# Mixer input projection as two panels of seven half-size products each

## The chip, the cores and the metric

The kernel runs on one core of a Trainium2 chip. The metric is device time in microseconds (us) of one execution of the whole program; the median of several executions is given with the lowest and the highest. The profile that is read below is of one further execution.

## The reference, cut to what matters

The program computes a block with a mixer (a gated linear attention beside a pooling branch), a mixture of 32 experts, and a second, two-layer block. The change touches one matrix product near the start, the mixer's input projection. `h` has 512 tokens, the context `hc` has 256, both with 1024 features.

```python
p_x = modulate(rmsnorm(h, norm_mix_w[l]), sh1, sc1) @ w_in[l]
p_c = modulate(rmsnorm(hc, norm_mix_w[l]), csh1, csc1) @ w_in[l]
q, k, v, g, r_f, r_b, pool_in = jnp.split(p, SPLIT_POINTS, axis=-1)
# widths: q 256, k 256, v 512, g 512, r_f 16, r_b 16, pool_in 512
gk_f = jax.nn.log_sigmoid((r_f @ w_gk_f + b_gk_f)) / GATE_NORMALIZER
```

Of the context only k, v and the two r are used. The same stage also needs the modulation vectors, `silu(c) @ w_ada + b_ada`, with `w_ada` of 1024 x 6144, of which 4096 columns are read here.

## The kernel before

Every weight comes through `ring`, a ring of slots of 1 MB each (128 partitions x 2048 floats). In this stage eight slots are used. The list of tiles is fixed when the program is built: `stream.add` appends a tile, tile n goes into slot n mod 8, and SyncE issues its load (`Stream.load`, line 188) as soon as tile n-8 has been given back. TensorE takes tiles in order with `take`; `release` gives the oldest back with a matmul, `owe` leaves that to the next `release` or `settle`, `keep` holds a tile a step longer. Tiles 0 to 7 are w_ada for the first modulation vectors, tiles 8 to 11 are w_in columns 0 to 1023 (q, k, then v), tile 12 is the upper half of w_in for g, 13 to 16 are w_ada, 17 is the lower half for g, 18 to 21 are w_ada, 22 to 31 are the same for the pooling input.

All of it is issued on SyncE's queue (q1 in the profile). GpSimd issues three transfers on its own queue (q0): x and ctx at the start and, at line 733, one store of 20352 KB of zeros to `y_scratch` in HBM, which is needed much later, by the experts. All queues use the same 16 DMA engines.

The stage runs on TensorE in this order. The normalised rows are transposed and written as `hT` (features on partitions, 512 + 256 columns). `project` (line 388) then goes over the eight feature chunks of 128, and for each over its output banks in PSUM, with one float32 matmul each (the profile counts each float32 matmul as two):

- q and k: four banks of 512 tokens and two of 256 context tokens; then the narrow product with `wr` (line 891) for r, and its copy `rT`;
- v: six banks (four of tokens, two of context). Ahead of feature chunks 1 to 4, `gates(i)` (line 902) puts in two small products of rT, into banks 0 and 1, which VectorE empties into `zb` (line 823);
- g: four banks; the pooling input: four banks. Ahead of each of their 16 feature chunks stands one step of `vector_step` (line 543): four matmuls side by side on quarters of the array, which multiply one w_ada tile by the vector.

ScalarE and VectorE empty the banks. ScalarE also turns `zb` into exponentials (lines 773 to 777, then `act_power`), VectorE scans it, and `dve_shift` and `dve_scale` make the operands of the gated linear attention, which starts in the next block, behind a barrier of all engines.

A product in seven parts is used in this kernel already, later, in the two last layers. One 1024 x 1024 weight panel, as four blocks of 512 x 512 named 11, 12, 21, 22, times 512 tokens in two halves of 256: instead of eight half-size products there are seven (`Panel`: p1, p2, p6, p7, p5, p4, p3), whose operands are four sums of feature quarters (`Sums`: s1 to s4) and four sums of weight blocks (`weights_t3`, `t2`, `t4`, `t1`, in place in the ring, lines 488 to 508). `channel_product` (line 453) is one such product with channels on partitions, 16 matmuls of 256 columns; `token_product` (line 440) has tokens on partitions, 8 matmuls of 512 columns.

## Time and profile before

| | us |
|---|---|
| median of 3 runs (lowest, highest) | 2169.72 (2169.31, 2170.83) |
| time of the profiled execution | 2184.99 |
| its span | 2182.8 |
| the stage of the change, on TensorE | 47.97 to 207.68 |

Times of instructions are in us from the start of the span. "Idle before" is the time in which the engine had nothing to do, with what ended it behind the arrow. In a window a digit such as PEclk 1.00 is the share of TensorE's full clock (2.4 GHz) that was granted, and DMA share is the mean busy share of the 16 DMA engines.

### The profile page before, as it was taken

What the parts mean: (1) busy time and instruction counts of PE and PEld (TensorE: products, weight loads), DVE (VectorE), ACT (ScalarE), POOL (GpSimd) and SP (SyncE); (2) the same over time, 40 slices, a digit from 0 to 9 for tenths busy, and PEclk for the clock granted to TensorE, in tenths of its full rate; (3) what the DMA queues carried; (4) which work ended last, traced back from release to release, by engine and by line L of the source; (5) the groups of instructions that cost most, each with busy time, mean ns of one, the idle gap of its engine ahead of it and who ended that gap; (6) DMA issues with size and microseconds to landing.
All of it is one profiled execution on the core that took longest, in us unless ns stands there. A gap on an engine that the chain in (4) does not pass through costs nothing.

```text
span 2182.8 us, 35887 instructions
## 1 busy us (share of the span) xinstructions
PE 2114.5 (97%) x14889; PEld 1141.3 (52%) x14889; DVE 950.8 (44%) x1640; ACT 491.0 (22%) x876; POOL 216.2 (10%) x266
## 2 busy tenths in 40 slices
PE   5999899999999999999999999899999999999998
PEld 2434545344444544444354443588584448777643
DVE  1041625833223223322322344754577625597742
ACT  2030312111101101110110110311126102666560
POOL 1000001121121122112112232200000000000000
PEclk9999999999999999999999999999999999999999
DMA  9957137999999999999999999723121032212200
GB/s 378 351 193 258 61 119 315 422 415 400 409 410 407 414 413 409 416 413 415 411 416 413 410 420 419 292 78 109 39 101 54 1 105 79 97 58 97 97 20 38
DMA packets 111830, 565.88 MB, mean 259 GB/s; under 512 B 16933, under 2 KB 29010, under 8 KB 77938
## 3 DMA queue, kind: packets, MB, share of 16 engines
q1 hardware_dynamic: 88950, 512.93, 58.4%
q0 software_dynamic: 19584, 49.84, 6.4%
q10 hardware_dynamic: 3228, 2.17, 0.3%
q8 instruction: 47, 0.77, 0.1%
q14 instruction: 21, 0.17, 0.0%
HBM read 545.21 MB, written 37.62 MB: 267 GB/s over the span
## 4 chain that ended last, share of the span: by engine, by line
PE 80%; DVE 3%; DMA 3%; issue 1%; ACT 1%; ACTq 0%; SPq 0%; DVEq 0%; POOLq 0%
PE ps L2309 30%; PE ps L459 11%; PE ps L2279 11%; PE ps L3848 5%; PE ps L3747 4%; PE ps L2287 4%; PE ps L447 3%; PE ps L1533 2%; PE ps L3727 2%; PE ps L3279 1%; DMA ring<-in_w_gu 1%; PE ps L3270 1%; DMA ring<-in_odd_w_in 1%; PE ps L2899 1%; PE ps L2943 1%
## 5 line engine op out<-in xcount | busy, mean ns | idle before, releaser
L2309 PE MATMUL ps<-ring,xeT 128*32 128x512 f32 x6144 | 684.5, 593 | 3.0 <-issue 1.7
L2309 PEld LDWEIGHTS ps<-ring,xeT 128*32 128x32 f32 x6144 | 259.9, 110 | 392.4 <-issue 335.5
L2279 PE MATMUL ps<-ring,mT 128*32 128x512 f32 x2048 | 322.3, 592 | 0.0
L2287 PE MATMUL ps<-ring,mT 128*32 128x256 f32 x2048 | 264.1, 379 | 0.0
L2048 DVE TENSOR_TENSOR mT<-ps,spread_bias 128x768 f32<-128x768 f32 x32 | 30.6, 957 | 462.5 <-PE ps L2309 462.4
L1986 ACT ACTIVATE mT<-mT 128x768 f32<-128x768 f32 x32 | 27.0, 845 | 867.0 <-DVE mT L2048 838.4
L2287 PEld LDWEIGHTS ps<-ring,mT 128*32 128x32 f32 x2048 | 118.3, 110 | 96.7 <-issue 66.2
L459 PE MATMUL ps<-hT_late,ring 128*128 128x256 f32 x704 | 155.5, 379 | 1.1 <-issue 1.1
L2279 PEld LDWEIGHTS ps<-ring,mT 128*32 128x32 f32 x2048 | 122.9, 110 | 52.8 <-issue 9.2
L459 PEld LDWEIGHTS ps<-hT_late,ring 128*128 128x128 f32 x704 | 133.4, 190 | 22.2 <-issue 4.1
L3848 PE MATMUL ps<-ring,mT 128*128 128x512 f32 x256 | 110.4, 592 | 0.0
L1808 POOL DMA_INDIRECT xe<-xn_scratch,idx x93 | 96.6, 1038 | 30.6 <-issue 28.7
L1819 ACT ACTIVATE xeT<-xturned,modx 128x96 f32<-128x96 f32 x248 | 91.8, 453 | 9.7 <-PE ps L2309 9.7
L2075 DVE STREAM_TRANSPOSE mT<-mT 128x768 f32<-128x768 f32 x31 | 30.3, 978 | 142.0 <-PE ps L2287 141.9
L3848 PEld LDWEIGHTS ps<-ring,mT 128*128 128x128 f32 x256 | 48.6, 190 | 60.8 <-issue 60.7
L1839 POOL TENSOR_TENSOR mark<-cst 128x1 f32<-128x1 f32 x57 | 11.9, 210 | 686.9 <-DVE ysb L2087 643.8
L402 PE MATMUL ps<-ring,hT 128*128 128x512 f32 x160 | 71.7, 598 | 0.0
L402 PE MATMUL ps<-hT,ring 128*128 128x512 f32 (+1 forms) x160 | 64.5, 556 | 2.2 <-DVE vtok L840 1.5
L1533 PE MATMUL ps<-ring,mixT 128*128 128x512 f32 x128 | 56.7, 596 | 2.4 <-DMA ring<-in_w_out 1.2
L1922 POOL DMA_INDIRECT y_scratch<-ysb,y_idx x54 | 55.6, 1029 | 23.1 <-issue 23.1
L459 PE MATMUL ps<-mT,ring 128*128 128x256 f32 x256 | 56.6, 379 | 0.0
L3747 PE MATMUL ps<-ring,mT 128*128 128x512 f32 x128 | 55.3, 592 | 0.0
(497 smaller groups left out, 2467.6 us busy)
## 6 DMA issues: line engine op xcount, KB each, us to landing
ring<-in_w_gu SPq DMA_DIRECT2D x128, 2048.0 KB, 9.4
ring<-in_w_down SPq DMA_DIRECT2D x128, 1024.0 KB, 28.2
y_scratch<-zeros POOLq DMA_DIRECT2D x1, 20352.0 KB, 99.1
ring<-in_even_w_in SPq DMA_DIRECT2D x18, 1024.0 KB, 7.3
ring<-in_w_ada SPq DMA_DIRECT2D x32, 512.0 KB, 8.0
ring<-in_odd_w_in SPq DMA_DIRECT2D x16, 1024.0 KB, 6.7
ring<-in_w_ada SPq DMA_DIRECT2D x8, 1024.0 KB, 20.1
ring<-in_w_in SPq DMA_DIRECT2D x8, 1024.0 KB, 18.4
```

Of the source, the lines that this page charges most:

```text
L402: mm = nc.tensor.matmul(dst, left(k, w, kk), right(k, w, kk), start=first, stop=last)
L447: mm = nc.tensor.matmul(out, left[:, k, t * P:(t + 1) * P], w[:, k, :], start=fresh and k == 0 and (n == BANK or t == 0), stop=k == 3, ski ...
L459: mm = nc.tensor.matmul(out, w[:, k, c * P:(c + 1) * P], left[:, k, :], start=fresh and k == 0 and c % 2 == 0, stop=k == 3, skip_group_che ...
L1533: mm = nc.tensor.matmul(bank(j_out[t, h].bank), mixT[:, k, t * P:(t + 1) * P], tiles[k // 2][:, k % 2, h * BANK:(h + 1) * BANK], start=k = ...
L1808: nc.gpsimd.indirect_dma_start(xe[:, q * DQ:(q + 1) * DQ], None, quarter_rows, bass.IndirectOffsetOnAxis(ap=idx[:, q:q + 1], axis=0), boun ...
L1819: nc.scalar.activation(xeT[:, j, 0:CAP].rearrange("p (q s) -> p q s", q=3), xturned[:].rearrange("p (q j s) -> p j q s", q=3, j=KD)[:, j], ...
L1922: nc.gpsimd.indirect_dma_start(y_parts[n], bass.IndirectOffsetOnAxis(ap=y_idx[:, n:n + 1], axis=0), src, None, bounds_check=(2 + 2 * n) * ...
L2279: mm = nc.tensor.matmul(quad(b, 2 * q + n), acted(k, q, src), w[:, kk, n * BANK:(n + 1) * BANK], start=first, stop=last)
L2287: mm = nc.tensor.matmul(quad(b + 1, c, 256), acted(k, 2, src), w[:, kk, c * 256:(c + 1) * 256], start=first, stop=last)
L2309: mm = nc.tensor.matmul(quad(q, c), left(q), part_columns(w, c), start=start, stop=stop)
L3747: mm = nc.tensor.matmul(bank(b), left[:, k, t * P:(t + 1) * P], w[k // 4][:, k % 4, :], start=fresh and k == 0, stop=k == KD - 1, skip_gro ...
L3848: return nc.tensor.matmul(bank(j.bank), mT[:, k, t * P:(t + 1) * P], w[:, k % 2, h * BANK:(h + 1) * BANK], start=k == 0, stop=k == 2 * KD - 1)
```

## The change

The q, k, v, g and pooling columns become two panels of 1024 columns: q, k with g, and v with the pooling input. Each is computed for the 512 tokens in seven half-size products; the context's k and v are products of their own (`context_keys`, `context_values`), each in two halves of the features. GpSimd makes the four feature sums, VectorE the eight weight sums, and results that two products share are copied by ScalarE and joined by VectorE. The four weight blocks of a panel now stand together in the list, ahead of the eight w_ada tiles, and the eight vector steps of a panel follow it in one go (`vector_cluster`). r and its gates come first. `weights`, `sums_ready` and a new signal `context` are made here instead of later.

```diff
-        add_panel(w_in, KD, 4, 0, 512)
-        add_panel(w_in, KD, 4, 512, 1024)
-        for c0, firsts in ((1024, (2 * D, 5 * D)), (1568, (3 * D, 4 * D))):
+        EARLY_ORDER = ("12", "11", "21", "22")
+        early_at = []
+        for sides, firsts in (((0, 1024), (2 * D, 5 * D)), ((512, 1568), (3 * D, 4 * D))):
+            early_at.append(len(stream.tiles))
+            for b in EARLY_ORDER:
+                k0, c = 4 * (b[0] == "2"), sides[b[1] == "2"]
+                add(ktiles(w_in, k0, 4, c, c + BANK), 4, BANK)
             for k in range(KD):
-                if k % 4 == 0:
-                    add(ktiles(w_in, k, 4, c0, c0 + 512), 4, 512)
                 stream.add(ada_pieces(k, *firsts), (2, D))
...
@@ GpSimd, after the store of zeros is issued
+                a21 = early.s3
+                early.ready["s1"] = sums_ready.on(nc.gpsimd.tensor_tensor(early.s1, a21, early.a22, ALU.add))
+                sums_ready.wait(pool)
+                early.ready["s2"] = sums_ready.on(nc.gpsimd.tensor_tensor(early.s2, early.s1, early.a11, ALU.subtract))
+                j_r.filled(pool)
+                j_rc.filled(pool)
+                early.ready["s3"] = sums_ready.on(nc.gpsimd.tensor_tensor(early.s3, early.a11, a21, ALU.subtract))
+                sums_ready.wait(pool)
+                early.ready["s4"] = sums_ready.on(nc.gpsimd.tensor_tensor(early.s4, early.a12, early.s2, ALU.subtract))
...
@@ VectorE, in its order
+                w = {b: arrived(dve, blocks(p_qkg, b)) for b in EARLY_ORDER}
+                weights_t3(dve, p_qkg, w)
                 j_r.filled(dve)
...
+                dve.wait_ge(context.sem, 1)
+                weights_t2(dve, p_qkg, w)
                 dve.wait_ge(gk_step.sem, 1)
                 z_half.on(nc.vector.tensor_scalar(zb, zb, 0.0, 1.0 / 16, ALU.min, ALU.mult))
                 z_half.wait(dve)
+                join_queries_and_keys(p_qkg.p2, p_qkg.p1, "11")
+                j_kc.filled(dve)
+                weights_t4(dve, p_qkg, w)
                 dve.wait_ge(gk_step.sem, 3)
...
+                weights_t1(dve, p_qkg, w)
...
-                for t, j in enumerate(j_v + j_vc):
-                    j.filled(dve)
-                    j.empty(nc.vector.tensor_copy(vtok[:, t, :], bank(j.bank)))
                 dve_shift(dve, 1)
+                join_22(dve, p_qkg, g_part["22"], by_channel(p_qkg.p5))
+                join_queries_and_keys(p_qkg.p4, p_qkg.p6, "21")
                 dve_scale(dve, 0)
                 dve_scale(dve, 1)
+                w = {b: arrived(dve, blocks(p_vp, b)) for b in EARLY_ORDER}
+                weights_t3(dve, p_vp, w)
                 j_gates.filled(dve)
                 j_gates.empty(nc.vector.tensor_copy(gate_rows, bank(j_gates.bank)))
+                dve.wait_ge(context.sem, 2)
+                weights_t2(dve, p_vp, w)
...
@@ TensorE (the three calls of project after the r product are gone too)
-                project(pe, 2, [(j, bank(j.bank), lambda k, w, kk, i=i: w[:, kk, i * P:(i + 1) * P],
-                                 lambda k, w, kk: hT[:, k, 0:T]) for i, j in enumerate(j_qk)]
...
+                def rest_of_panel(p, product, b):
+                    pe.wait_ge(weights.sem, p.ready["t2"])
+                    pe.wait_ge(sums_ready.sem, early.ready["s2"])
+                    product(pe, p.p6, early.s2, b["11"], False)
+                    pe.wait_ge(sums_ready.sem, early.ready["s3"])
+                    product(pe, p.p7, early.s3, b["12"], True)
+                    stream.owe()
+                    pe.wait_ge(weights.sem, p.ready["t1"])
+                    product(pe, p.p5, early.s1, b["11"], False, True)
+                    stream.owe()
+                    product(pe, p.p4, early.a22, b["21"], False, True)
+                    stream.owe()
+                    pe.wait_ge(sums_ready.sem, early.ready["s4"])
+                    product(pe, p.p3, early.s4, b["22"], False, True)
+                    stream.owe()
+
+                def vector_cluster(job):
+                    for k in range(KD):
+                        mm = vector_step(pe, job, k, take(pe).rearrange("p c n -> p (c n)"))
+                        if k < KD - 1:
+                            stream.release(mm)
+                    stream.owe()
+                    job.done(mm)
+
+                b = {"12": take(pe), "11": take(pe)}
+                channel_product(pe, p_qkg.p1, early.a11, b["11"], True, True)
+                context_keys(0, b["11"])
+                for i in range(4):
+                    gates(i)
+                b["21"] = take(pe)
+                channel_product(pe, p_qkg.p2, early.a12, b["21"], True)
+                context_keys(1, b["21"])
+                b["22"] = take(pe)
+                rest_of_panel(p_qkg, channel_product, b)
+                vector_cluster(j_gates)
+                b = {"12": take(pe), "11": take(pe)}
+                token_product(pe, p_vp.p1, early.a11, b["11"], True, True)
+                context_values(0, b["11"])
+                b["21"] = take(pe)
+                token_product(pe, p_vp.p2, early.a12, b["21"], True)
+                context_values(1, b["21"])
+                b["22"] = take(pe)
+                rest_of_panel(p_vp, token_product, b)
+                vector_cluster(j_rows2)
```

A last argument of True makes the first matmul of a product settle what is owed. After the change tiles 8 to 11 are blocks 12, 11, 21, 22 of the first panel, 12 to 19 are w_ada, 20 to 23 the blocks of the second panel, 24 to 31 w_ada.

## Rows read from the trace of the kernel before

**Rows 1.** The page, part 4: shares of the chain that ended last.
```profile
PE 80%; DVE 3%; DMA 3%; issue 1%; ACT 1%; ACTq 0%; SPq 0%; DVEq 0%; POOLq 0%
```

**Rows 2.** Windows: stretch, length, busy us of each engine, PEclk, DMA share, GB/s.
```profile
47.97:82.55 34.58, 34.58 (x97) 18.16 (x97) 0.00 (x0) 2.56 (x5) 0.00 (x0) 1.00 1.02 377
82.55:85.26 2.71, 2.71 (x33) 0.93 (x32) 0.69 (x1) 0.48 (x2) 0.00 (x0) 1.00 1.00 319
85.26:131.82 46.56, 46.56 (x116) 21.20 (x113) 15.44 (x15) 12.14 (x6) 0.00 (x0) 1.00 0.86 285
131.82:207.68 75.86, 74.36 (x257) 25.43 (x256) 16.89 (x24) 8.92 (x15) 0.00 (x0) 1.00 0.59 215
```

**Rows 3.** Timeline of TensorE in the stage: start, length, line, shapes.
```profile
90.52 1.45 PE L902 MATMUL ps<-rT,wgk 128*128 128x512 f32 x4
91.81 5.31 PE L402 MATMUL ps<-ring,hT 128*128 128x512 f32 x12
...
138.22 1.07 PE L543 MATMUL ps<-ring,scol 128*32 128x512 f32 x8
...
142.84 1.06 PE L543 MATMUL ps<-ring,scol 128*32 128x512 f32 x8
```

**Rows 4.** Chain in order of time (two late panels); timeline of TensorE (twelve quarter-array steps).
```profile
1583.62 48.36 PE ps L459 x224
...
1340.06 10.51 PE L2309 MATMUL ps<-ring,xeT 128*32 128x512 f32 x96
```

**Rows 5.** Timeline of VectorE, ScalarE and GpSimd.
```profile
91.58 1.14 DVE L823 TENSOR_SCALAR ring<-ps,vec 128x512 f32<-128x512 f32 x2 [5.75 <-PE ps L902]
...
112.07 2.77 ACT L773 ACTIVATE res<-ring 128x3072 f32<-128x3072 f32 x1 [29.04 <-DVE ring L823]
...
123.10 3.36 DVE L829 SCALAR_TENSOR_TENSOR ring<-res,ring 128x3072 f32<-128x3072 f32 x1 [6.47 <-ACT res L777]
...
285.75 0.62 POOL L1367 TENSOR_TENSOR ring<-ring,mod 128x256 f32<-128x256 f32 x1 [12.28 <-DMA ring<-in_w_router]
```

**Rows 6.** Groups by form, VectorE, 1404 to 1620: weight sum of one block.
```profile
L490 DVE TENSOR_TENSOR ring<-ring 128x2048 f32<-128x2048 f32 x3 | 6.9, 2284 | 0.0
```

**Rows 7.** SyncE's issues in the timeline; its waits over 40 to 210.
```profile
83.62 0.38 SPq L188 DMA_DIRECT2D ring<-in_w_in  x1
110.03 43.92 SPq L188 DMA_DIRECT2D ring<-in_w_ada  x8
...
SPq L188 <- PE ps L402: 111.2, 7, 26.0
```

**Rows 8.** Transfers issued in 41:42, 83:84 and 174.5:174.6: KB each, us to landing.
```profile
y_scratch<-zeros POOLq DMA_DIRECT2D x1, 20352.0 KB, 99.1
...
ring<-in_w_in SPq DMA_DIRECT2D x1, 1024.0 KB, 22.4
...
ring<-in_w_in SPq DMA_DIRECT2D x1, 1024.0 KB, 8.6
```

**Rows 9.** DMA queues (packets, MB, share): both in 48:64, q1 in 84:104 and 112:124.
```profile
q0 software_dynamic: 852, 3.49, 55.8%
q1 hardware_dynamic: 907, 3.04, 46.9%
...
q1 hardware_dynamic: 517, 1.03, 13.3%
...
q1 hardware_dynamic: 278, 1.02, 21.5%
```

**Rows 10.** One window, columns as in rows 2.
```profile
80.00:112.00 32.00, 32.00 (x108) 14.80 (x107) 5.65 (x10) 2.44 (x5) 0.00 (x0) 1.00 1.01 329
```

**Rows 11.** TensorE before and after an idle stretch: timeline, then one window.
```profile
222.77 3.70 PE L1213 MATMUL ps<-ring,ptok 128*128 128x512 f32 x8
...
239.09 5.05 PE L1213 MATMUL ps<-ring,ptok 128*128 128x512 f32 x8
...
238.00:240.00 2.00, 2.00 (x13) 1.36 (x12) 0.74 (x2) 0.93 (x1) 0.00 (x0) 0.50 0.00 0
```

More of the change, by code:

```diff
@@ L659, in build @@
         gla_done = signal("gla_done")
+        weights, sums_ready, context = signal("weights"), signal("sums_ready"), signal("context")
+        quarter = lambda ap: ap.rearrange("p (k n) -> p k n", k=4)
+        early = Sums(hT[:, 0:4, 0:HALF], hT[:, 4:KD, 0:HALF], hT[:, 4:KD, HALF:T], quarter(scratch[:, 6144:7168]),
+                     quarter(scratch[:, 7168:8192]), hT[:, 0:4, HALF:T], quarter(g2b[:]), {})
+        qk_part = {"11": (qT[:, :, 0:HALF], kT[:, :, 0:HALF]), "21": (qT[:, :, HALF:], kT[:, :, HALF:T])}
+        g_part = {"12": sgT[:, :, 0:HALF], "22": sgT[:, :, HALF:]}
+        v_part = {"11": vtok[:, 0:2, :], "21": vtok[:, 2:4, :]}
+        pool_part = {"12": ptok[:, 0:2, :], "22": ptok[:, 2:4, :]}
         def gset(i):
@@ L824, in _, with join_queries_and_keys @@
                                                         ALU.add))
+                def join_queries_and_keys(j, copied, b):
+                    j.filled(dve)
+                    copied.emptied_for(dve)
+                    both, (q, k) = by_channel(j), qk_part[b]
+                    nc.vector.scalar_tensor_tensor(out=q, in0=both[:, 0:2, :], scalar=DK ** -0.5, in1=q, op0=ALU.mult,
+                                                   op1=ALU.add)
+                    j.empty(nc.vector.tensor_tensor(k, k, both[:, 2:4, :], ALU.add))
+                dve.wait_ge(context.sem, 1)
+                weights_t2(dve, p_qkg, w)
                 dve.wait_ge(gk_step.sem, 1)
@@ L903, in gates @@
                                                 rT[:, cols], start=True, stop=True))
-                project(pe, 2, [(j, bank(j.bank), lambda k, w, kk, t=t: hT[:, k, tokens(t)],
-                                 lambda k, w, kk: w[:, kk, :]) for t, j in enumerate(j_v + j_vc)],
-                        before={k: lambda k=k: gates(k - 1) for k in range(1, 5)})
-                project(pe, 2, [(j, bank(j.bank), lambda k, w, kk, i=i: w[:, kk, i * P:(i + 1) * P],
-                                 lambda k, w, kk: hT[:, k, 0:T]) for i, j in enumerate(j_g)],
-                        before=vector_between(pe, j_gates))
@@ L911, in _, with context_keys @@
-                project(pe, 2, [(j, bank(j.bank), lambda k, w, kk, t=t: hT[:, k, tokens(t)],
-                                 lambda k, w, kk: w[:, kk, :]) for t, j in enumerate(j_pool)],
-                        before=vector_between(pe, j_rows2))
+                def context_keys(half, w):
+                    if half == 0:
+                        j_kc.open(pe)
+                    for i in range(2):
+                        for k in range(4):
+                            mm = nc.tensor.matmul(ps[:, j_kc.bank, i * TC:(i + 1) * TC], w[:, k, (2 + i) * P:(3 + i) * P],
+                                                  hT[:, 4 * half + k, T:], start=half == i == k == 0, stop=half == 1 and k == 3,
+                                                  skip_group_check=True)
+                    if half:
+                        j_kc.done(mm)
+                    else:
+                        context.on(mm)
@@ new lines, in context_values @@
+                def context_values(half, w):
+                    if half == 0:
+                        j_vc.open(pe)
+                    for t in range(NTC):
+                        for k in range(4):
+                            mm = nc.tensor.matmul(ps[:, j_vc.bank + t, :], hT[:, 4 * half + k, tokens(NT + t)], w[:, k, :],
+                                                  start=half == k == 0, stop=half == 1 and k == 3, skip_group_check=True)
+                    if half:
+                        j_vc.done(mm)
+                    else:
+                        context.on(mm)
@@ L2721, in build @@
             nyquist = stat[:, 0:KD]
[L2722 removed]
+            opened = again(powers)
             gate_first = psum.job(6, "act", (7,))
```

65 lines of the change are left out of this document (42 added, 23 removed).

## Prediction, before the change was run

> **What bounds the kernel now.** I read the chain of waits first: four fifths of it is TensorE [rows 1], so matmul time taken away inside the chain is worth its full length, as long as nothing else comes last there. Then the windows over the stage: from 47.97 to 207.68, 159.71 us, TensorE is busy throughout but for 1.5 us, at full clock [rows 2]. The stage is TensorE's now. The same rows show the second resource: the DMA engines are full in the first two windows (share 1.02 and 1.00), 0.86 in the third and only 0.59 in the last. What fills them is the store of zeros, 20352 KB issued at 41.47, which takes 99.1 us, until 140.6 [rows 8]. SyncE in turn waits 111.2 us for slots that the projections give back [rows 7]: transfers are late because slots are, and today that costs nothing, since w_ada tiles are wanted one by one, each beside 3.4 us of other matmuls [rows 3].
>
> **TensorE's work after the change.** A full 512-column float32 matmul takes 0.86 us, a 256-column one 0.43 (the 34.58 us of the first window hold 32 of the one and 16 of the other) [rows 2]. Now the projections are 128 matmuls for tokens, 16 small ones for the context's k and 16 full ones for its v: 110 + 6.9 + 13.8 = 130.7 us. After: each panel is seven products of 16 x 0.43. The same product in a late panel measures 48.36 us for seven [rows 4], so two panels are 96.7, and with the context 117.4. Saved: 13.3 us.
>
> Two orders change as well. A vector step between projections costs 4.62 - 3.44 = 1.18 us (138.22 to 142.84, less eight records of 0.43) [rows 3]; steps back to back, of the same quarter-array shape, cost 10.51/12 = 0.88 [rows 4]. Sixteen steps: 18.9 becomes 14.0, 4.9 saved. The four gates cost 1.29 each between feature chunks (90.52 to 91.81), 5.2 in all [rows 3]. Now they stand back to back and share banks 0 and 1, so each waits for VectorE to empty the first: filled 1.06 after the start, 0.75 of emptying (of the 1.14 for both) [rows 5], a signal, about 1.9 a turn: 3 x 1.9 + 1.3 = 7.0, 1.8 lost. The 1.5 us of waiting at line 402 goes. With the r product (2.7) the stage would be 2.7 + 117.4 + 7.0 + 14.0 = 141.1 us against 159.7: **18.6 us less, if nothing is waited for**.
>
> **Do the sums hide?** GpSimd: 256 columns took 0.62 us [rows 5], so 1024 take at most four times that, 2.5 (a linear estimate). s1 and s2 from 48 end by 53, s3 and s4 by 59; p6 needs s2 at 78. Were they four times slower, s2 would still come at 68. A weight sum on VectorE takes 2.28 us [rows 6]. My clock for the first panel: r 47.97 to 50.7, p1 57.6, context 61.0, gates 68.0, p2 74.9, context 78.4, p6 85.3, p7 92.2, p5 99.1, p4 106.0, p3 112.9. t3 runs at 48, ahead of the copies of rT, and delays them to about 51; the gates need them at 61. t2 stands behind the last gate's emptying: 69.2 + 2.3 = 71.5, wanted 78.4. ScalarE's exponentials start when zb is full and end 11.0 later (112.07 to 123.10 [rows 5]), at 80.2; VectorE then has 3.4 for line 829 and t1 behind p6, 85.3 + 2.3 = 87.6, wanted at 92.2. In the second panel the context's products stand in the same places and are twice as long. If any of these covers failed, the delay would be of 1 to 5 us, once. None is charged.
>
> **The transfers.** This is where I part from the sum above. The four blocks of a panel hold four of eight slots until p7, p5, p4 and p3 are through. So w_ada tiles 16, 17 and 18 can be asked for only at 92.2, 99.1 and 106.0, and tiles 19 to 23, the last w_ada tile and the whole second panel, only as the vector steps give slots back, at 113.8 (19 and 20), 114.7 (21), 115.6 and 116.4. The vector steps end at 119.9 at best; then p1 of the second panel wants tiles 20 and 21 at once, where the kernel now wants a tile every few us from stock.
>
> At 114 the zeros are still in flight: the DMA engines are full until 112 [rows 10], and moved 54% zeros after it (the last ended at 140.6). Up to tile 21 the bytes from 48 on are 20.8 MB of zeros, some 3.1 of tiles already asked for, and 6.3 of tiles 16 to 21: 30.2 MB. At the 409 GB/s of 48:64 (6.53 MB in 16 us [rows 9]) that is 74 us, at the 329 of 80:112 [rows 10] 92 us: 122 to 140, with perfect balance over the engines. The old order had carried only tiles up to 18 when the zeros were through.
>
> How the two queues share: with both full, 48 to 64, the ring got 3.04 MB, 190 GB/s [rows 9]. But one block asked for at 83.62 [rows 7] took 22.4 us [rows 8], while the ring moved 1.03 MB in 20 us [rows 9]; and the tile asked for at 110.03 [rows 7] moved its 1.02 MB over the time to 124 [rows 9]. A block of w_in arrives in rows of 2 KB, half as long as those of w_ada and of the zeros, so it gets less per turn, and a tile has landed only when the slowest of 16 engines is through. Tile 18, asked at 106, should land at about 120 like the one of 110. Then 19, 20 and 21 follow, 3.15 MB. Bound below: at 190 GB/s throughout, 16.6 us, 137; with tile 18 in early and no slow engine, 133. Bound above: tiles 20 and 21 at about 91 GB/s (half of 190, for the half rows) are 23 us behind 5.5 for tile 19, 148.5; the zeros, pushed back by the added ring traffic from 140.6 to about 148, then free the engines, so 152 at most. I take **146**, near the upper end, since the row nearest to it is the 22.4 us of a single w_in block.
>
> **The sum.** The second panel starts at 146 instead of 119.9. From there it has 48.4 of products, 13.8 of context values and 7.0 of vector steps, 69.2 us; block 22 for t3 lands by about 153, t2 follows at 159, wanted at 173. After so long an idle stretch TensorE comes back at half clock: behind a wait of 3 us a group of 3.70 us took 5.05, at a granted 0.50 [rows 11]; with the shorter groups beside it about 3 us are lost. 146 + 69.2 + 3 = 218.2 against 207.68: +10.5 us. The last w_ada tile, asked for one step into the last vector steps, is wanted 6.2 us later, which an unhindered MB about meets: 0 to 2 us more, not charged. The start of the next block shifts as it is. Profiled time 2184.99 + 10.5 = 2195.5; the runs' median is 15.3 us lower than the profiled time, and the same difference on it gives **2180.2**, 0.5% more.
>
> **Rivals.** (a) *Even sharing.* If the queues share each engine turn by turn whatever the row length, the three tiles land at 137, the stage ends at 137 + 69.2 + 3 = 209.2: +1.5 us, 2171; with 133 instead, -2.5. For it speaks 48 to 64 (55.8 to 46.9% [rows 9]), against it the 22.4 us. The Trainium skill (DMA: Bandwidth & Descriptors, "Queues, rings and completion order") says that every DMA engine goes round-robin between queues that have work, a packet at a time; the stretch from 48 to 64 agrees and that from 84 to 104 does not, at 13.3%. Chance 0.27, the point of decision being tile 21 at 135.5.
> (b) *The transfers are hidden* (the other sign). If the zeros, with the ring silent from 68 to 92, were through by 114, a third tile in line would land 8.6 us after its issue, as at 174.5 [rows 8]: 123.3, stage end about 193.5, -14 us, 2156; down to 2151 with nothing waited for. Against it: full DMA engines from 80 to 112, and byte counts that reach 122 only at the best rate. Chance 0.15, for anything under -4.3 us.
> (c) *Worse than I say*: tile 21 only when the zeros are wholly through and at 152 or later, or a second stall in panel two: +17 us and more, 2187 and up. Chance 0.06.
> That leaves 0.52 for my forecast, +4 to +16, whose own range is 2174 to 2186.
>
> **Numbers.** Within 0.2% (4.3 us, about what a measurement of this kernel can tell from no change) lies most of (a). Faster by more 0.17, same 0.26, slower 0.57. The range takes in (a) and the near part of (c), and stops short of most of (b): 2163 to 2188.
>
> **What the profile will show.** TensorE idle before L543 near 116 to 120 and before L447 near 146, both put down to DMA of the ring; SyncE's waits for slots at 92 to 117; zeros landing after about 105 us; L459 and L447 products of 6.9 us; gates 1.9 us apart; no wait for VectorE or GpSimd at p6, p5 or p3; a granted clock of 0.50 after the long wait. I am wrong if tile 21 lands before 135, that is if the ring gets half of the engines or more from 107 on, or if the zeros end by 120.

## The result, and the profile after

The changed kernel takes 2180.47 us (median of 6, 2178.17 to 2184.59), the kernel before, on the same chip, 2170.16 (6 runs, 2168.80 to 2172.30): 1.0051 of the time before, 95% interval 1.0039 to 1.0063, or some 10 us more. The profiled execution has a span of 2178.0 us and a time of 2179.86.

The timeline of TensorE in the changed kernel, over the stage; columns are start, length, engine, line, operation and shapes, and in brackets the idle time before with what ended it:

```profile
48.74 2.79 PE L951 MATMUL ps<-hT,wr 128*32 128x512 f32 x32 [0.71 <-ACT hT L792]
51.45 7.17 PE L461 MATMUL ps<-hT,ring 128*128 128x256 f32 x32
58.47 3.62 PE L970 MATMUL ps<-hT,ring 128*128 128x256 f32 x16
61.92 1.45 PE L962 MATMUL ps<-rT,wgk 128*128 128x512 f32 x4
63.88 1.53 PE L962 MATMUL ps<-rT,wgk 128*128 128x512 f32 x4 [0.50 <-DVE ring L865]
...
107.29 7.07 PE L461 MATMUL ps<-g2b,ring 128*128 128x256 f32 x32
114.29 5.36 PE L545 MATMUL ps<-ring,scol 128*32 128x512 f32 x48
123.25 1.94 PE L545 MATMUL ps<-ring,scol 128*32 128x512 f32 x8 [3.60 <-DMA ring<-in_w_ada]
129.52 1.94 PE L545 MATMUL ps<-ring,scol 128*32 128x512 f32 x8 [4.33 <-DMA ring<-in_w_ada]
146.69 9.03 PE L449 MATMUL ps<-ring,hT 128*128 128x512 f32 x16 [15.24 <-issue]
155.57 7.03 PE L983 MATMUL ps<-ring,hT 128*128 128x512 f32 x16
...
210.59 7.34 PE L545 MATMUL ps<-ring,scol 128*32 128x512 f32 x64
219.17 0.85 PE L1261 MATMUL ps<-cst,ring 128*128 128x128 f32 x6 [1.24 <-PEq L731]
```

One reads three waits down the right margin: six of the eight vector steps run, the seventh and the eighth each wait for their w_ada tile, and then TensorE stands for 15.24 us ahead of the second panel. Nothing else in the stage waits for more than 0.50 us. The releaser of the long wait is given as "issue", which names no culprit. The transfers name it: the first product wants blocks 12 and 11 (tiles 20 and 21), and tile 21, issued at 119.73, needs 26.9 us. SyncE's issue, then the transfer issued in 119.7:119.8 (KB, us to landing):

```profile
119.73 2.23 SPq L188 DMA_DIRECT2D ring<-in_w_in  x1
...
ring<-in_w_in SPq DMA_DIRECT2D x1, 1024.0 KB, 26.9
```

It lands at 146.6, and the product starts at 146.69. The same 0.1 us between the landing of the second block and the start of the second panel is found in every run below that waits at this point. The next block starts at 219.17, against 208.89 before: 10.3 us later.

Windows of the same trace; columns as in [rows 2]:

```profile
48.74:217.90 169.16, 144.41 (x576) 84.09 (x576) 54.85 (x46) 28.32 (x29) 11.31 (x4) 0.92 0.70 245
131.45:146.69 15.24, 0.01 (x1) 0.03 (x1) 0.00 (x0) 0.00 (x0) 0.00 (x0) 0.50 0.78 271
146.69:147.69 1.00, 0.99 (x2) 0.48 (x3) 0.00 (x0) 0.00 (x0) 0.00 (x0) 0.50 0.99 291
```

Before, TensorE was busy but for 1.5 us of this stage, at full clock [rows 2]. Now it is busy 144.4 of 169.2 us, at a mean granted clock of 0.92, and the share of the chain that ended last is 75% TensorE and 6% DMA where it was 80% and 3% [rows 1]. After the wait it comes back at 0.50 (1.2 GHz), so that the first product takes 9.03 us instead of 7.03.

The rest of this execution gives back and takes a little. From the start of the next block to the first expert products is 146.58 us (219.17 to 365.75) where it was 148.07 (208.89 to 356.96), 1.5 less. From the first to the second full group of expert products it is then 1.6 us more (26.44 for the 24.86 from 356.96 to 381.82 before):

```profile
365.75 10.51 PE L2429 MATMUL ps<-ring,xeT 128*32 128x512 f32 x96
...
392.19 10.51 PE L2429 MATMUL ps<-ring,xeT 128*32 128x512 f32 x96 [0.40 <-DVE mT L2169]
```

10.3 - 1.5 + 1.6 = 10.4 us up to that point, beside 10.3 between the medians. The agreement is closer than one execution allows: with the sums on VectorE (below) the same stretch takes 150.78 us instead of 146.58, at the same ratio of medians. From there the two shown profiles differ by some 15 us the other way, and that is not the change; the run of the kernel before once more, below, points to the chip.

### The profile page after: what moved, and what is told of

It is laid out like the page before. It is cut to its first block, busy times and chain, and to the rows that moved or that the text cites. A ratio compares the mean times of both kernels' runs of the same rounds, so it can differ in the third digit from the quotient of the medians.

```text
span 2178.0 us, 36119 instructions
## 1 busy us (share of the span) xinstructions
PE 2084.0 (96%) x14969; PEld 1027.8 (47%) x14969; DVE 971.2 (45%) x1647; ACT 495.2 (23%) x878; POOL 226.9 (10%) x270
## 4 chain that ended last, share of the span: by engine, by line
PE 75%; DMA 6%; DVE 3%; issue 1%; ACT 1%; ACTq 0%; POOL 0%; SPq 0%; DVEq 0%; POOLq 0%
PE ps L2429 27%; PE ps L461 11%; PE ps L2399 9%; PE ps L3968 5%; PE ps L3867 4%; PE ps L2407 4%; PE ps L449 3%; PE ps L1653 2%; PE ps L3847 2%; DMA hT_late<-y_scratch,dest 2%; DMA ring<-in_w_down 1%; DMA ring<-in_w_gu 1%; PE ps L3399 1%; PE ps L3390 1%; DMA ring<-in_odd_w_in 1%
## 5 line engine op out<-in xcount | busy, mean ns | idle before, releaser
L2429 PE MATMUL ps<-ring,xeT 128*32 128x512 f32 x6144 | 668.1, 593 | 5.6 <-DMA ring<-in_w_gu 3.9
L2429 PEld LDWEIGHTS ps<-ring,xeT 128*32 128x32 f32 x6144 | 196.6, 110 | 447.8 <-issue 441.0
L2399 PE MATMUL ps<-ring,mT 128*32 128x512 f32 x2048 | 266.6, 592 | 0.2 <-DMA ring<-in_w_down 0.2
L2407 PE MATMUL ps<-ring,mT 128*32 128x256 f32 x2048 | 157.4, 379 | 0.0
L461 PEld LDWEIGHTS ps<-hT_late,ring 128*128 128x128 f32 x704 | 135.0, 192 | 22.4 <-issue 3.7
L2407 PEld LDWEIGHTS ps<-ring,mT 128*32 128x32 f32 x2048 | 66.6, 110 | 153.1 <-issue 153.1
L2399 PEld LDWEIGHTS ps<-ring,mT 128*32 128x32 f32 x2048 | 66.5, 110 | 57.6 <-issue 18.5
L492 DVE TENSOR_TENSOR ring<-ring 128x2048 f32<-128x2048 f32 (+1 forms) x10 | 23.6, 2363 | 79.3 <-DMA ring<-in_w_in 38.7
L461 PEld LDWEIGHTS ps<-mT,ring 128*128 128x128 f32 x256 | 48.6, 190 | 6.6
## 6 DMA issues: line engine op xcount, KB each, us to landing
y_scratch<-zeros POOLq DMA_DIRECT2D x1, 20352.0 KB, 103.2
ring<-in_w_ada SPq DMA_DIRECT2D x32, 512.0 KB, 11.5
```

The source lines that it names most:

```text
L461: mm = nc.tensor.matmul(out, w[:, k, c * P:(c + 1) * P], left[:, k, :], start=fresh and k == 0 and c % 2 == 0, stop=k == 3, skip_group_che ...
L2399: mm = nc.tensor.matmul(quad(b, 2 * q + n), acted(k, q, src), w[:, kk, n * BANK:(n + 1) * BANK], start=first, stop=last)
L2407: mm = nc.tensor.matmul(quad(b + 1, c, 256), acted(k, 2, src), w[:, kk, c * 256:(c + 1) * 256], start=first, stop=last)
L2429: mm = nc.tensor.matmul(quad(q, c), left(q), part_columns(w, c), start=start, stop=stop)
```

## The experiments

Each edit is against the changed kernel where nothing else is said. Ratios are to the kernel before on the same chip, in the same session, with a 95% interval.

### The sums on VectorE

```diff
@@ GpSimd: the four sums go; VectorE, behind the copies of rT
+                early.ready["s1"] = sums_ready.on(nc.vector.tensor_tensor(early.s1, a21, early.a22, ALU.add))
...
+                early.ready["s4"] = sums_ready.on(nc.vector.tensor_tensor(early.s4, early.a12, early.s2, ALU.subtract))
```

> The changed kernel with the four feature sums on VectorE, behind the copies of rT, instead of on GpSimd. My theory: the sums are hidden on either engine (s2 is wanted at 79), so the time is the same within 2 us of 2180; the weight sum t3 takes 2.3 us instead of 4.1, as nothing on GpSimd runs beside it. Rival, that GpSimd beside VectorE and beside the store of zeros costs: several us faster, and the zeros end earlier.

2180.87 us (4 runs, 2180.37 to 2183.77), ratio 1.0051 (1.0034 to 1.0068): the same ratio as the changed kernel's, as expected, and the rival of several us is out. The second panel starts at 146.20, the next block at 219.22. First GpSimd and VectorE in the changed kernel, then VectorE in this one:

```profile
48.77 2.36 POOL L757 TENSOR_TENSOR ring<-hT 128x1024 f32<-128x1024 f32 x1 [3.44 <-ACT hT L792]
51.21 4.29 POOL L759 TENSOR_TENSOR ring<-ring,hT 128x1024 f32<-128x1024 f32 x1
...
49.17 4.11 DVE L492 TENSOR_TENSOR ring<-ring 128x2048 f32<-128x2048 f32 x1 [0.56 <-DMA ring<-in_w_in]
```
```profile
49.66 2.29 DVE L492 TENSOR_TENSOR ring<-ring 128x2048 f32<-128x2048 f32 x1 [0.66 <-DMA ring<-in_w_in]
...
52.80 1.22 DVE L851 TENSOR_TENSOR ring<-hT 128x1024 f32<-128x1024 f32 x1
```

A sum takes 2.36 us on GpSimd and 1.22 on VectorE. The placing on GpSimd has a cost of its own that is easily seen here: the weight sum t3, started 0.4 us into a GpSimd sum, takes 4.11 us instead of 2.29, and the GpSimd sum that follows takes 4.29 instead of 2.36, as if each waited for the other. The Trainium skill (SBUF — State Buffer, "SBUF: two separate sides") says that VectorE with two SBUF inputs, beside a GpSimd operation that reads SBUF, shares a port pair with it by a lock held for a whole instruction. These lengths agree: the GpSimd sum ends at 51.13, and 2.29 behind it is 53.42, where t3 ends at 53.28; 2.36 behind that is 55.64, where the second GpSimd sum ends at 55.50. None of it reaches TensorE in either kernel: the sums are hidden wherever they are made.

### The whole store of zeros a block later, in both kernels

```diff
@@ GpSimd, the stage of the change
-                rows_zeroed.on(pool.dma_start(y_dram..., zeros...), 16)
-                rows_zeroed.wait(pool)
@@ GpSimd, start and end of the next block
                 for a in amat:
                     amat_zero.on(nc.gpsimd.memset(a, 0.0))
+                rows_zeroed.on(pool.dma_start(y_dram..., zeros...), 16)
...
                 xn2_stored.wait(pool)
+                rows_zeroed.wait(pool)
```

The changed kernel with it:

> The changed kernel, with the store of zeros issued in the next block instead of ahead of the first panel (waited for one block later). My theory, that the second panel waits because its four blocks are asked for only from 114 on and then share the DMA engines with the zeros: tile 21 lands about 9 us after its issue, near 124, the second panel starts there instead of at 146.7, the stage ends near 194 instead of 217.9, and the whole is 10 to 20 us faster than the changed kernel (less what the zeros cost in the next block), 2160 to 2171. Rival, that the late asking alone makes the wait and the zeros don't matter: the second panel still starts near 140, the whole stays at about 2178.

The kernel before with it:

> The kernel before, with the same move of the store of zeros. Both theories: its stage does not wait for transfers, so it still ends near 207.7; what differs from 2170 is the price of the zeros in the next block, where the matmuls are short and w_out is waited for: 0 to 8 us, 2170 to 2178. The difference of this run and the changed kernel with the same move is then the worth of the product in seven parts without the collision: 13 to 14 us by my theory, about -8 (slower) by the rival.

2196.92 us (4 runs, 2193.51 to 2197.89), ratio 1.0122 (1.0105 to 1.0139), and 2204.03 (2203.65 to 2206.50), ratio 1.0162 (1.0145 to 1.0179). Both totals missed, for one reason that the expectations had put far too low. TensorE, then the waits of GpSimd and TensorE over 200 to 310 (us in total, times, longest), in the changed kernel with the late store:

```profile
124.71 9.82 PE L449 MATMUL ps<-ring,hT 128*128 128x512 f32 x16 [4.41 <-issue]
...
197.94 0.85 PE L1260 MATMUL ps<-cst,ring 128*128 128x128 f32 x6 [1.23 <-PEq L731]
```
```profile
POOL posm L1483 <- POOLq L1079: 95.4, 1, 95.4
...
PE ps L1653 <- PEq L1079: 35.8, 1, 35.8
```

The stage did what the theory says: the second panel starts at 124.71 instead of 146.69 and the next block at 197.94 instead of 219.17, 21.2 us earlier (2.5 of them were gained ahead of the stage, which starts at 46.21 here and at 48.74 there). But the store, issued at 199.5 and 98.3 us long, ends at about 298, and the block in which GpSimd waits for it does not end before: TensorE stands 35.8 us at the barrier (36.1 in the kernel before), and the other compute engines are idle but for 0.7 us of ScalarE. That wait ends about 98 us behind each stage's end, so the difference of the stages stays: the next blocks start at 197.94 and 209.07, 11.1 us apart (2.0 of them from the start of the stage, 46.21 and 48.16), and the medians are 7.1 apart, where 13 to 14 were expected of this pair and -8 by the rival. In the kernel before the stage itself does not gain (next block at 209.07, 208.89 before): without the zeros there is nothing in it to win.

### The store in two halves

```diff
-                zeros[0:CAP, :]...to_broadcast([CAP, (E + XB) * D // BANK, BANK])), 16)
+                y_dram...[:, 0:53, :], zeros[0:CAP, :]...to_broadcast([CAP, 53, BANK])), 16)
@@ GpSimd, start of the next block
+                y_dram...[:, 53:106, :], zeros[0:CAP, :]...to_broadcast([CAP, 53, BANK])), 16)
@@ GpSimd, end of the next block
+                rows_zeroed.wait(pool)
```

The changed kernel with it, and the kernel before with it:

> The changed kernel with the store of zeros cut in two halves of 10176 KB: the first is issued where the whole store was, the second at the start of the next block's GpSimd part, and GpSimd waits for each within its own block. Nothing is left out. My theory: the second panel waits because the zeros share the transfer engines with SyncE's loads until about 140 us. With half of them gone the first half lands at about 90 to 95 us (the whole took 99.1 us for 20352 KB), so that from then on the loads have the engines alone; the tile that the second panel's first product needs then lands between 122 and 128 instead of about 146, the stage ends between 194 and 199 instead of 217.9, and the second half, issued at about 198 and needing some 50 us, lands before that block's end at about 262, so that the block's end does not wait, as it did when the whole store was moved: 2156 to 2163 us in all, 8 to 14 less than before the change. Rival: late release of the ring's slots is what delays the tile, and the zeros hardly matter: the second panel starts after 138 and the time stays between 2174 and 2181. Second rival: the second half lands later than the next block's end, or slows that block's own loads: the stage ends near 197 but the time lies at 2165 or above.

> The kernel before the change with the same split of the zeros, and nothing else. Nothing is left out. In it no tile was late in this stage but one wait of some 1.5 us, so I expect no difference: 2168 to 2171 us, the stage ending at 206 to 208. If the second half of the zeros costs the next block something (the second rival of the run beside this one), it shows here alone: 2173 or more.

The changed kernel: 2178.59 us (5 runs, 2177.31 to 2179.68) where the kernel before took 2185.70 on this chip (21 runs), ratio 0.9965 (0.9952 to 0.9979). The kernel before with the same split: 2188.07 (10 runs, 2185.62 to 2191.24), ratio 1.0010 (1.0001 to 1.0020), 2.4 us more, so the split alone wins nothing. The expected 8 to 14 us less came out as 7.1 less, although the second panel and the end of the stage came within the times expected. The second half of the zeros, 57.5 us long, lands at 258.7, and TensorE goes from the next block into the one behind it at 265.67, after 1.18 us of waiting: no barrier waits for the store. The timeline of the changed kernel with the split:

```profile
121.93 1.07 PE L545 MATMUL ps<-ring,scol 128*32 128x512 f32 x8 [1.54 <-DMA ring<-in_w_ada]
127.41 8.64 PE L449 MATMUL ps<-ring,hT 128*128 128x512 f32 x16 [4.41 <-issue]
...
199.55 0.85 PE L1264 MATMUL ps<-cst,ring 128*128 128x128 f32 x6 [1.23 <-PEq L731]
```

With the half store gone by the time the blocks are asked for, the second panel starts 19.3 us earlier (146.69 to 127.41) and the next block 19.6 (219.17 to 199.55). The transfers say the same. The DMA queues over 104 to 124 us (packets, MB, share of the 16 engines), and the loads of the second panel's blocks with KB each and median us to landing, first in the changed kernel, then with the split:

```profile
q0 software_dynamic: 885, 3.60, 51.7%
q1 hardware_dynamic: 1020, 3.49, 45.6%
...
ring<-in_w_in SPq DMA_DIRECT2D x4, 1024.0 KB, 26.9
```
```profile
q1 hardware_dynamic: 1568, 4.31, 60.4%
...
ring<-in_w_in SPq DMA_DIRECT2D x4, 1024.0 KB, 10.7
```

The second block takes 26.9 us with the zeros beside it (the first 22.4, the third 27.2, the fourth is not recorded) and 10.7 without (the only one of the four with a recorded landing). The zeros also delay the asking. SyncE's issues of the four blocks, in the changed kernel and with the split:

```profile
117.92 17.83 SPq L188 DMA_DIRECT2D ring<-in_w_in  x4
```
```profile
116.15 4.91 SPq L188 DMA_DIRECT2D ring<-in_w_in  x4
```

The issues alone take 17.8 us instead of 4.9, so tile 21 is asked for at 119.73 instead of 116.64 though its slot comes free at about the same time. What the split leaves, 1.54 and 4.41 us of waiting, is the ring: the blocks are asked for only at 116.15 to 117.98.

### The kernel before once more

> The kernel before, unchanged, for one more profile. Its shown profile had an expert stage some 13 us longer than all profiled kernels of this study, and a time of 2184.99 us beside a median near 2170. If that was an accident of this execution, this one has about 1786 us from the first full group of expert products to the end, as the others, and about 2170 us in all; if the change makes the experts faster (another place of the kernel's code, other tiles in the ring), it again has about 1800.

2185.42 us, on a chip where 21 runs of the kernel before had a median of 2185.70. The second full group of expert products, in this run and in the changed kernel with the split, on the same chip:

```profile
382.49 10.51 PE L2309 MATMUL ps<-ring,xeT 128*32 128x512 f32 x96 [0.40 <-DVE mT L2049]
```
```profile
374.90 10.51 PE L2433 MATMUL ps<-ring,xeT 128*32 128x512 f32 x96 [0.40 <-DVE mT L2173]
```

From there to the end of the span (2183.2 and 2175.4) are 1800.7 and 1800.5 us, as in the shown profile of before (381.82 to 2182.8, 1801.0). On the other chips it is 1785.8 in the changed kernel and 1785.9 with panels first. So the 15 us depend on the chip, and neither theory of the expectation was right: not one odd execution, and not the code. The chip of the shown profile is not on record; that it was this one is inferred from the 1801.0. All runs here are therefore read as ratios to the kernel before on their own chip.

### The order of tiles in the ring

Both panels first, all sixteen vector steps behind them (in this and the next edits the PSUM bank of the first vectors and its copy by VectorE move behind the second panel too, not shown):

```diff
             for b in EARLY_ORDER:
                 ...
                 add(ktiles(w_in, k0, 4, c, c + BANK), 4, BANK)
+        for firsts in ((2 * D, 5 * D), (3 * D, 4 * D)):
             for k in range(KD):
                 stream.add(ada_pieces(k, *firsts), (2, D))
...
-                vector_cluster(j_gates)
                 b = {"12": take(pe), "11": take(pe)}
...
                 rest_of_panel(p_vp, token_product, b)
+                vector_cluster(j_gates)
                 vector_cluster(j_rows2)
```

> The changed kernel, zeros where they were, but the second panel's four blocks stand right behind the first panel's in the ring, and all sixteen vector steps follow the second panel. My theory: the blocks are asked for by 50, no wait ahead of the second panel, which runs from about 114 to 176; then nine of the w_ada tiles have yet to come, at about 2.6 us each, so that the stage ends near 202 to 204; whole time 2164 to 2168. Rival, that the sums or VectorE hold up the second panel: still a wait of tens of us ahead of its products.

2172.72 us (10 runs, 2170.71 to 2175.21), ratio 1.0011 (1.0001 to 1.0021): the panel ran as expected, the total missed by some 5 us. The same order with the store in two halves:

> The changed kernel with the second panel's four blocks right behind the first's in the ring, all sixteen vector steps last, and the zeros split as in the run beside it. Nothing is left out. With the unsplit zeros its last vector steps waited for their w_ada tiles and the stage ended at about 205.4. If it was the zeros that made those tiles late, the steps now run without a wait and the stage ends between 192 and 197, the time at 2155 to 2163. If the late release of the slots alone makes them late (the sixteen w_ada tiles can only be asked for when the second panel's blocks are given back), the stage still ends at 203 or later, the time at 2169 to 2173, and the order with vector steps between the panels is the better one once the zeros are out of the way.

2187.07 (10 runs), ratio 1.0002 (0.9993 to 1.0012), the outcome that was put down to the slots. The timeline of panels first, with the zeros whole:

```profile
114.08 7.11 PE L450 MATMUL ps<-ring,hT 128*128 128x512 f32 x16 [1.21 <-ACT sgT L534]
...
182.97 1.06 PE L546 MATMUL ps<-ring,scol 128*32 128x512 f32 x8 [0.71 <-DMA ring<-in_w_ada]
186.12 1.93 PE L546 MATMUL ps<-ring,scol 128*32 128x512 f32 x8 [2.09 <-DMA ring<-in_w_ada]
...
204.40 1.07 PE L546 MATMUL ps<-ring,scol 128*32 128x512 f32 x8 [0.92 <-DMA ring<-in_w_ada]
206.70 1.51 PE L1262 MATMUL ps<-cst,ring 128*128 128x128 f32 x6 [1.23 <-PEq L732]
```

The second panel no longer waits for a block: in the ring it stands ahead of the w_ada tiles and was loaded long before. Instead the last nine vector steps wait, one every 2.6 us, each for a tile of 1 MB, with the DMA engines full (share 1.03 and 405 GB/s over 186 to 204). With the zeros in halves nine steps wait just so and the next block starts at 208.24. Here the zeros play no part; the slots do: w_ada tiles are asked for only as the second panel gives its slots back. The stage ended at 205.5, 1.5 us behind the expected 202 to 204, and another 2.2 us went in the next block (150.24 us to the first expert products, 148.07 before) and 1.7 between the first two groups of them.

Four vector steps between the panels and twelve behind, zeros whole; then five and eleven, and six and ten, with the zeros in halves:

```diff
+            if sides[0] == 0:
+                for k in range(4):
+                    stream.add(ada_pieces(k, *firsts), (2, D))
...
                 rest_of_panel(p_qkg, channel_product, b)
+                vector_cluster(j_gates, 0, 4)
...
-                vector_cluster(j_gates)
+                vector_cluster(j_gates, 4)
                 vector_cluster(j_rows2)
```

> The changed kernel with the zeros where they were, and only the order of tiles and steps changed: four vector steps between the panels, the second panel, then the other twelve. The second panel's blocks are now tiles 16 to 19 of the ring instead of 20 to 23, so that they are asked for when the first panel's blocks go (92 to 114 us) and not when vector tiles go. Nothing is left out. My theory (late requests and the zeros together delay the blocks): the first two blocks land before or near 118, the second panel starts at 117 to 120 (146.7 in the changed kernel) though the zeros still run until 140; the four tiles that can only be asked for after the second panel's end, at about 187, come at 2.6 us each, so that the stage ends between 197 and 202: 0.995 to 0.998 of the time before. Rival (it is the zeros alone that hold the blocks back, whenever they are asked for): the second panel starts after 130, the stage ends at 206 or later, the ratio is 1.0 or more.

> Five vector steps between the panels, eleven behind, and the zeros in two halves. Nothing is left out. The second panel's first two blocks are asked for at about 99 and 106 and the engines are free of zeros from about 92: no wait of over 1.5 us ahead of the second panel. Three tiles are asked for after the second panel: the stage ends between 193 and 198, the ratio is 0.993 to 0.9955. If the ring's slots give less than that, the last vector steps wait for more than 6 us in all and the ratio is 0.9965 or more, no better than the split alone.

> The same with six vector steps between and ten behind. Nothing is left out. The first two blocks are asked for at about 106 and 114, so the second panel waits for up to 3 us, while only two tiles are asked for after it: the stage ends between 192 and 198, the ratio is 0.9925 to 0.9955, within 0.001 of the run with five.

| | second panel starts | wait ahead of it | next block | median (runs) | ratio |
|---|---|---|---|---|---|
| four and twelve, zeros whole | 125.46 | 8.62 | 210.38 | 2173.99 (11) | 1.0016 (1.0007 to 1.0025) |
| five and eleven, halves | 117.72 | 0 | 197.37 | 2163.17 (6) | 0.9965 (0.9953 to 0.9977) |
| six and ten, halves | 120.00 | 1.00 | 196.72 | 2161.68 (5) | 0.9954 (0.9941 to 0.9968) |

The kernel before took 2170.70 on that chip. The three kernels enter the stage 0.7 to 1.1 us earlier than the changed one. The timeline of four and twelve; then its loads of the first two blocks of the second panel (issued at 93.01 and 99.92); then, in the changed kernel, the second halves of the two w_ada tiles asked for at the same points (tiles issued at 94.11 and 101.01, each as two transfers of 512 KB, the second some 0.4 us behind the first):

```profile
125.46 10.16 PE L453 MATMUL ps<-ring,hT 128*128 128x512 f32 x16 [8.62 <-issue]
...
199.28 1.06 PE L549 MATMUL ps<-ring,scol 128*32 128x512 f32 x8 [1.52 <-DMA ring<-in_w_ada]
```
```profile
ring<-in_w_in SPq DMA_DIRECT2D x1, 1024.0 KB, 20.5
...
ring<-in_w_in SPq DMA_DIRECT2D x1, 1024.0 KB, 25.5
```
```profile
ring<-in_w_ada SPq DMA_DIRECT2D x1, 512.0 KB, 16.6
...
ring<-in_w_ada SPq DMA_DIRECT2D x1, 512.0 KB, 15.3
```

A tile of w_ada (rows of 4 KB) is there 17.0 and 15.7 us after it was asked for, a block of w_in (rows of 2 KB) after 20.5 and 25.5.

The expectation for four and twelve missed: blocks asked for 20 to 25 us earlier (93.01 and 99.92) arrive 21 us earlier, and still too late, because beside the zeros a block takes 20.5 us (the next one, 25.5). Its rival (the zeros alone) missed the start as well, which moved from 146.69 to 125.46, but the stage's end and the ratio are those that it named: the last four vector steps wait 5.4 us, and the first product at half clock takes 10.16 us for 7.03. Both parts are needed: zeros out of the way or an early request each bring the start of the second panel some 20 us forward, and both together take the wait away. With five and eleven it is the tail that waits, four steps of 0.28 to 1.75 us for tiles asked for late, 5.1 us in all; its stage ended as expected, but its ratio missed the 0.993 to 0.9955 and is the 0.9965 that was named for no gain over the split. "Six and ten" came as expected, with a ratio at the upper end. These two stages ended 22 us earlier than the changed kernel's, and the medians are 7.5 and 9.0 us under the kernel before: 3 to 4 us short of the stages' gain of 11.5 and 12.2, most of which again goes into the next block (149.4 and 150.4 us to the first expert products, 148.1 before) and the way to the second group of them (1.6 and 1.8). The interval of "six and ten" lies under 1 by 0.0032 at least, and its ratio is the lowest of the study. But the split alone, with the order of the changed kernel, had 0.9965 (0.9952 to 0.9979): the three are not told apart by their times. That the new order adds to the split is seen in the stage alone (next block at 196.72 and 197.37 for 199.55), by 2 to 3 us.

## Why the prediction was right, step by step

| step of the prediction | said | the profile after |
|---|---|---|
| work without waits | 141.1 us | 142.0 |
| gates | 1.9 a turn | 1.96 to 2.03 (61.92, 63.88, 65.91, 67.94) |
| back-to-back vector steps | 0.88 each | 0.89 and 0.92 (5.36 for six, 7.34 for eight) |
| sums and weight sums | hidden | hidden; GpSimd 2.36 us |
| tile 18 lands | about 120 | 123.2 |
| tile 21 asked for | 114.7 | 119.73 |
| tile 21 in flight | 31.3 us | 26.9 us |
| the second panel starts | 146 | 146.69 |
| loss by the clock | 3 us | 2.0 in p1, 2.0 in the two late steps |
| stage, from there to its end | 72.2 | 71.2 (146.69 to 217.9) |
| zeros end | about 148 | 145.3 (42.10 + 103.2) |
| total | 2180.2 | 2180.47 |

**The work.** The 142.0 is 169.2 less the waits (3.60, 4.33, 15.24), less 2.0 and 2.0 for groups at half clock (9.03 for 7.03, and twice 1.94 for 0.92). So TensorE's work fell by 159.7 - 142.0 = 17.7 us, where 18.6 was worked out (the savings that the prediction lists one by one, 13.3 + 4.9 - 1.8 + 1.5, add up to 17.9); 27.2 of waits and low clock less 17.7 is the stage's 9.5, and it started 0.8 later. The sum was right in what it counted and in counting it apart from the transfers; the kernels with five or six steps between, which wait 5.1 and 4.3 us in the places named, got 11.5 and 12.2 of it.

**The long wait.** It was put at 119.9 to 146, and is 119.65 to 146.69, with 2 x 1.94 us of vector steps inside. That the zeros and the late slots make it is shown, not argued: take the zeros away (124.71), halve them (127.41) or ask earlier (125.46), and the second panel starts 19 to 22 us sooner; halve them and ask earlier, and at most 1.00 us of waiting is left ahead of it. The waits themselves, 23.2 us in the changed kernel, are 5.7, 6.0 and 8.6 us in the first three; the rest of the shift is low clock, the earlier start of the stage and, in the third, four vector steps that stand behind the panel. The prediction saw one idle stretch ahead of the vector steps and one ahead of the panel; there were two ahead of the last two vector steps, 7.9 us, before the 15.24, because tiles 18 and 19 were each 3 to 4 us later than put down. That changed nothing of the end, since tile 21 decides it.

**The landing of tile 21 was right in its number and wrong in its working: the 146 is in good part luck.** Tile 21 was asked for 5.0 us later than put down and was in flight 4.4 us less, two errors that cancel; and 146 was picked by judgement within 133 to 152. The prediction let tiles 19, 20 and 21 come one behind the other, with the last two at 91 GB/s because their rows are half as long. The transfers of the changed kernel over 118 to 146.5 and over 124 to 144 (queue q1 is the ring's, q0 the zeros'):

```profile
q1 hardware_dynamic: 2481, 5.75, 56.0%
q0 software_dynamic: 760, 3.07, 30.9%
```
```profile
q1 hardware_dynamic: 1827, 3.77, 51.0%
q0 software_dynamic: 533, 2.14, 31.5%
```

In those 28.5 us the ring moved 5.75 MB, 202 GB/s, not 91; 3.15 MB would have been done in 16 us, at 134. But the loads issued behind tile 21, blocks 22 and 23, were under way at the same time: when it landed, 2.6 MB more had moved than the 3.15 (the rest of tile 18 among them). And the 16 engines were only 0.78 busy in the wait, so there were empty engines while the block was not there. Whether the loads behind took turns from it, or a few engines were late with their share of it while the others went on, no run tells. The prediction's upper bound, 28.5 us for 3.15 MB with the last two tiles at 91 GB/s, stands in fact for 28.5 us with 5.75 MB at 202 GB/s. What was right in it is that a block of w_in is slow beside the zeros, slower than a tile of w_ada (20.5 and 25.5 us for 17.0 and 15.7). How much of that is the row length, and how much the loads that are issued behind, no run took apart.

**The rivals.** (a) would have had tile 21 at 137 or before, and it landed at 146.6; yet the queues did share about evenly, 51.7 to 45.6% of the engines in 104 to 124, and over 107 to 146.6 the ring had 52.6% of them. The prediction named that share (half or more from 107 on) as a sign that tile 21 lands before 135. The sign came and the landing did not follow: a share of engine time says little about when one transfer of several has landed. The turn-taking that the Trainium skill describes (DMA: Bandwidth & Descriptors, "Queues, rings and completion order") agrees with that stretch, and not with 94.2 to 104, where the ring had a single tile or two in flight and got 16.7% while the zeros had 83.2%. (b) needed the zeros through by 114; they ended at 145.3. (c) needed tile 21 at 152.

**What the correction stood for.** The 15.3 us between profiled time and runs was carried over as a constant. That was right for the median: the runs put the difference into the expert stage of another chip, behind the change.

## What to carry to other kernels

Fewer multiplications shorten a stage only as far as its loads come: here 17.7 us of TensorE work was saved and 27.2 of waiting and low clock bought, since a product in seven parts holds four of eight slots until its last parts, and its blocks are wanted at once instead of one by one. Before regrouping work, write down for each tile when its slot comes free, when it is wanted and what bulk transfer runs beside it; a bulk store whose result is needed much later is best cut in pieces that end within the block that waits for them, for moved whole it cost 36 us at the next barrier. And put some work that needs few tiles between two bursts that need many, to neither side too much.

## What the runs showed of the hardware

- A block of 1 MB in rows of 2 KB took 20.5 to 29.6 us beside the store of zeros (the second panel's blocks in the changed kernel and with four steps between), a tile in 4 KB rows 15.7 and 17.0; without the store the former took 10.7 with four of them in flight. Transfers behind it in the queue move at the same time (5.75 MB in 28.5 us, where 3.15 were wanted up to this block); that they delay its landing is not shown.
- Beside the zeros SyncE's four issues of 1 MB took 17.8 us, with the halved zeros gone 4.9.
- A block of the program with an unfinished store that GpSimd waits for ended with the store: 35.8 us in which TensorE stood.
- A GpSimd sum (1024 floats a partition, 2.36 us) and a VectorE sum with two inputs in SBUF (2.29 us) stretched each other to 4.29 and 4.11 us.
- The same program took 15 us more on one chip than on the others, all of it from the expert stage on, where the DMA engines are full (DMA share 0.99 from 382 to 1400 us in the shown profile of before).
- Left open: why it is 1.3 to 1.8 us more from the first to the second full group of expert products in every kernel of the changed form (26.1 to 26.7 us for 24.9). The place is the same in all nine: TensorE stops within the group behind these products, after 13 of its instructions, and waits for nothing that the profile shows. In the changed kernel:

```profile
377.40 1.91 PE L2429 MATMUL ps<-ring,xeT 128*32 128x512 f32 x13
379.86 4.48 PE L2429 MATMUL ps<-ring,xeT 128*32 128x512 f32 x35 [0.55 <-issue]
```
```profile
q8 instruction: 1, 0.02, 2.5%
```

The second fence is the queue of instructions over 376 to 378.5: one packet of 16 KB, at the start of this group in all nine. In the four profiles of the form before it comes 3 us later, and the group runs through. That would fit an engine that waits for its code, but it is not shown: another such packet, at 384.7, goes without a stop, and no run moved the code alone.
- Left open too: why the next block takes 0.5 to 3.5 us more in most of the changed kernels and 1.5 less in the profile of the changed kernel itself. Some enter it at half clock (first group 1.51 us for 0.85: panels first, and four, five or six steps between), but with the sums on VectorE the clock is full there and the block takes 2.7 us more as well.
